# Branch products of attention and merge as three products of rounded parts, in one step of a hybrid decoder on one Trainium2 core

## The reference

```python
n = rms_norm(x, ln1_g)
q_g, k_g, v_g, r_g, a_g, dil_qkv, q_m, gates = split_cols(n @ w_in)
og, gla_state = gla_chunked(qg, kg, vg, lg, gla_s0, gla_chunk)      # gated linear attention
br_gla = og.reshape(B, S, -1) @ w_br_gla                            # 1024 -> 1024
# dilated attention in three groups, mixed per head by the softmax of their denominators
od = jnp.sum(wts[..., None] * jnp.stack(outs, axis=0), axis=0)
br_dil = od.reshape(B, S, -1) @ w_br_dil                            # 512 -> 1024
br_mem = om.reshape(B, S, -1) @ w_br_mem                            # 512 -> 1024
gt = jax.nn.sigmoid(gates.reshape(B, S, N_BRANCH, D))
merged = gt[:, :, 0] * br_gla + gt[:, :, 1] * br_dil + gt[:, :, 2] * br_mem
h = x + merged @ w_out
y = h + peer(rms_norm(h, ln2_g), ...)                               # experts, gathered by row
```

## Time and profile before

| | us |
|---|---|
| median of three runs | 4821.14 |
| the profiled execution, its own time | 4822.78 |
| its span, first to last instruction | 4821.1 |
| PE busy | 4198.3 (87%) |
| VectorE busy | 2510.8 (52%) |
| ScalarE busy | 1744.3 (36%) |
| GpSimd busy | 1589.1 (33%) |
| mean granted clock of TensorE | 0.956 of full speed |

### The profile page before, as it was taken

The page is one execution under the profiler, slowest core; times in us unless marked ns, Lnnn a source line. Parts: engine busy times, 40 slices in busy tenths (PEclk is TensorE's granted clock), DMA queues, the critical chain, the costliest instruction groups (busy, mean ns, idle before and its releaser), DMA issues.

```text
span 4821.1 us, 55456 instructions
## 1 busy us (share of the span) xinstructions
PE 4198.3 (87%) x18644; PEld 2507.5 (52%) x18644; DVE 2510.8 (52%) x5454; ACT 1744.3 (36%) x4662; POOL 1589.1 (33%) x1435
## 2 busy tenths in 40 slices
PE   7999999997555988979889898898898898988987
PEld 6888888886434665444344344343443443443331
DVE  2111111117641763546666666666666666666665
ACT  2111111114411554324444444444444444444443
POOL 0000000004620541124444444444444444444443
PEclk9999999997677999989999999999999999999999
DMA  8898998882457773679999999999999999999998
GB/s 284 285 325 296 320 321 279 293 292 93 134 204 275 239 231 134 222 303 421 421 421 419 411 418 416 417 415 413 416 415 418 415 413 414 418 416 405 416 408 368
DMA packets 317403, 1642.14 MB, mean 341 GB/s; under 512 B 43832, under 2 KB 85656, under 8 KB 175224
## 3 DMA queue, kind: packets, MB, share of 16 engines
q0 software_dynamic: 164720, 1168.36, 59.2%
q1 hardware_dynamic: 116464, 248.64, 15.0%
q10 hardware_dynamic: 35984, 222.30, 13.7%
HBM read 1550.39 MB, written 318.03 MB: 388 GB/s over the span
## 4 chain that ended last, share of the span: by engine, by line
DMA 35%; PE 13%; issue 4%; ACT 4%; DVE 1%; POOL 0%; DVEq 0%; POOLq 0%; ACTq 0%; SPq 0%; PEldq 0%
DMA ex_rows<-scratch_uv,ex_E 35%; PE ex_ps_y L2674 11%; PE ex_ps_q L2622 1%; ACT ex_diag L2376 1%; ACT ex_w L2368 1%; PE ex_ps_t L2587 1%; ACT ex_gel L2364 1%; ACT L2364 0%; ACT L2359 0%; POOL ex_rows L2307 0%; PE ex_ps_y L2668 0%; DVE ex_dots L2521 0%; DVE ex_rows L2521 0%; ACT ex_ex L2359 0%; DMA ex_n2u<-scratch_h 0%
## 5 line engine op out<-in xcount | busy, mean ns | idle before, releaser
L2674 PE MATMUL ex_ps_y<-ex_rows,ex_diag 128*128 128x512 f32 (+1 forms) x4224 | 2030.0, 614 | 310.2 <-ACT ex_diag L2376 285.3
L2521 DVE CUSTOM_DVE_ANT_0 ex_rows<-ex_rows,ex_n2u 128x1024 f32<-128x1024 f32 x1056 | 1294.8, 1226 | 908.7 <-DMA ex_rows<-scratch_uv,ex_E 888.2
L2307 POOL DMA_INDIRECT ex_rows<-scratch_uv,ex_E x1056 | 1233.8, 1168 | 1548.3 <-PE ex_ps_y L2674 1402.9
L2674 PEld LDWEIGHTS ex_ps_y<-ex_rows,ex_diag 128*128 128x128 f32 (+1 forms) x4224 | 739.7, 189 | 1449.0 <-ACT ex_diag L2376 790.0
L2364 ACT ACTIVATE ex_gel<-ex_dots 128x1 f32<-128x1 f32 x1056 | 214.2, 203 | 1425.7 <-DVE ex_dots L2521 1423.1
L410 PE MATMUL pj_ps<-pj_w_hi,pj_nT 128*128 128x470 f32 x3072 | 699.5, 378 | 4.0 <-DVE pj_w_lo L246 2.8
L410 PEld LDWEIGHTS pj_ps<-pj_w_hi,pj_nT 128*128 128x128 f32 x3072 | 580.2, 189 | 87.6 <-issue 8.1
L274 DVE COPY pj_zo<-pj_ps 128x470 f32<-128x470 f32 x96 | 61.3, 646 | 698.8 <-PE pj_ps L410 494.4
L2376 ACT ACTIVATE ex_diag<-ex_ident,ex_w 128x128 f32<-128x128 f32 x1024 | 411.1, 401 | 33.5
L410 PE MATMUL pj_ps<-pj_w_lo,pj_nT 128*128 128x470 f32 x1536 | 362.2, 378 | 0.0
L274 ACT COPY pj_zo<-pj_ps 128x470 f32<-128x470 f32 x96 | 51.8, 553 | 807.1 <-PE pj_ps L410 450.7
(11 more groups left out here) (384 smaller groups left out, 3700.6 us busy)
## 6 DMA issues: line engine op xcount, KB each, us to landing
pj_w<-in_w_in POOLq DMA_DIRECT2D x24, 1880.0 KB, 17.7
scratch_z<-pj_zo SPq DMA_DIRECT2D x192, 235.0 KB, 11.9
scratch_uv<-in_peer_u ACTq DMA_DIRECT2D x8, 4096.0 KB, 25.1
scratch_uv<-in_peer_v ACTq DMA_DIRECT2D x8, 4096.0 KB, 42.5
scratch_uv<-in_peer_u ACTq DMA_DIRECT2D x4, 8192.0 KB, 41.6
scratch_uv<-in_peer_v ACTq DMA_DIRECT2D x4, 8192.0 KB, 72.8
out_dk_s<-in_cache_dil_k ACTq DMA_DIRECT2D x8, 4088.0 KB, 43.0
out_dv_s<-in_cache_dil_v ACTq DMA_DIRECT2D x8, 4088.0 KB, 54.7
```

What stands on the lines that cost most here:

```text
L2307: pool.indirect_dma_start(out=rows[:, p % SLOTS, :], out_offset=None, in_=d["uv"], in_offset=bass.IndirectOffsetOnAxis(ap=E[:, turn % 4, k ...
L2521: nc.vector.tensor_tensor_reduce(out=row, in0=row, in1=n2u[:, tile % 2], scale=1.0, scalar=0.0, op0=ALU.mult, op1=ALU.add, accum_out=dots[ ...
L2674: last = nc.tensor.matmul(y[0:n, 512 * c:512 * c + 512], diag[:, p % DIAGS, 0:n], rows[:, p % SLOTS, D + 512 * c:D + 512 * c + 512], start ...
```

## The change

The branch products of both stages become three products of rounded parts. The weights are no longer used from where they are loaded: w_br_gla goes into wo, and from there ScalarE copies each of its eight slices, rounded, to wb[0], and GpSimd writes the remainder to wb[1]. This is done in turns 1 to 4 by ScalarE (two slices at the end of a turn) and turns 2 to 5 by GpSimd (two slices at the head of a turn). w_br_dil and w_br_mem are then loaded into the two halves of wo at turns 7 and 15, and stay there until the merge, which begins by rounding them: eight copies by ScalarE, four remainders by VectorE and four by GpSimd.

The turned inputs are rounded by ScalarE's copy as before (to ogT[:, 0] and aT[.., 0]), and VectorE subtracts to get the remainder (ogT[:, 1], aT[.., 1]); PE waits for the remainder. The branch stream of attention begins at turn 3 and not 0, and so ends in turn 38; its 48 products a tile (24 for each half) are placed 0, 24, 9 and 15 in the four parts. w_out is not loaded in attention but in the merge, by SyncE at t = 4 ahead of the load of tile 6's rows.

```diff
@@ attend
-    wb = d["wb"] = d["hold_wb"].enter_context(nc.sbuf_tensor("wb", [P, 2 * KD, D], fp32))
+    wb = d["wb"] = [d["hold_wb"].enter_context(nc.sbuf_tensor(n, [P, KD, D], f32r)) for n in ("wb_hi", "wb_lo")]
+    FIRST_BRANCH = 3
+    SPLIT_AT = {n: range(2 * n - 2, 2 * n) for n in range(1, 5)}
+    TERMS = [(a, b, k) for a, b in ((0, 0), (1, 0), (0, 1)) for k in range(KD)]
@@ SyncE
-            weights = [(wb[:, 8:12], "w_br_dil", wb_in), (wb[:, 12:16], "w_br_mem", wb_in), (wo[:], "w_out", wo_in)]
+            weights = [(wo[:, 0:4], "w_br_dil"), (wo[:, 4:8], "w_br_mem")]
-            sp.dma_start(wb[:, 0:8], d["w_br_gla"].rearrange("(k p) n -> p k n", p=P)).then_inc(wb_in, 16)
+            sp.dma_start(wo[:], d["w_br_gla"].rearrange("(k p) n -> p k n", p=P)).then_inc(wb_in, 16)
-                if n % 8 == 7 and n // 8 < 3:
+                if n % 8 == 7 and n // 8 < 2:
+                    sp.wait_ge(wb_lo, KD)
@@ GpSimd
+            def split_weights(k):
+                pool.wait_ge(wb_hi, k + 1)
+                nc.gpsimd.tensor_tensor(wb[1][:, k], wo[:, k], wb[0][:, k], ALU.subtract).then_inc(wb_lo, 1)
             for n in range(LAST + 1):
+                for k in SPLIT_AT.get(n - 1, ()):
+                    split_weights(k)
@@ ScalarE
+            def split_weights(k):
+                act.wait_ge(wb_in, 16)
+                nc.scalar.copy(wb[0][:, k], wo[:, k]).then_inc(wb_hi, 1)
...
+                for k in SPLIT_AT.get(n, ()):
+                    split_weights(k)
@@ VectorE
+            def turned_branch(t, half):
+                dve.wait_ge(ogT_hi, 2 * t + half + 1)
+                ks = slice(4 * half, 4 * half + 4)
+                nc.vector.tensor_tensor(ogT[:, 1, ks, 0:width(t)], ps_b[:].rearrange("p (k t) -> p k t", k=4)[:, :, 0:width(t)],
+                                        ogT[:, 0, ks, 0:width(t)], ALU.subtract).then_inc(ogT_out, 1)
@@ TensorE
-                        pe.wait_ge(wb_in, 16)
+                        pe.wait_ge(wb_hi, KD)
+                if t == 0 and half == 0 and terms[0] == 2 * KD:
+                    pe.wait_ge(wb_lo, KD)
+                for i in terms:
+                    a, b, k = TERMS[i]
+                    last = nc.tensor.matmul(ps_b[0:width(t)], ogT[:, a, k, 0:width(t)], wb[b][:, k, 512 * half:512 * half + 512],
+                                            start=(i == 0), stop=(i == len(TERMS) - 1))
+                if part == 0 and place < 2:
+                    turn_branch(t, place)
                 elif part == 1:
-                    branch_product(t, 0, (range(2, 4), range(4, 5), range(5, 7))[place])
+                    branch_product(t, 0, (range(0, 8), range(8, 16), range(16, 24))[place])
+                elif part == 2 and place:
+                    branch_product(t, 1, (range(0, 4), range(4, 9))[place - 1])
+                elif part == 3:
+                    branch_product(t, 1, (range(9, 14), range(14, 19), range(19, 24))[place])
@@ merge
+                if t == 4:
+                    sp.wait_ge(dil_lo, 4)
+                    sp.wait_ge(mem_lo, 4)
+                    sp.dma_start(wo[:], d["w_out"].rearrange("(k p) n -> p k n", p=P)).then_inc(wo_in, 16)
                 if t + 2 < N:
                     load_a(t + 2)
@@ GpSimd, ahead of its tiles
+            for k in range(4, KD):
+                pool.wait_ge(wb_hi, 2 * (k - 4) + 2)
+                nc.gpsimd.tensor_tensor(wb[1][:, k], wo[:, k], wb[0][:, k], ALU.subtract).then_inc(mem_lo, 1)
@@ ScalarE, ahead of its tiles
+            act.wait_ge(wb_in, 48)
+            for k in (0, 4, 1, 5, 2, 6, 3, 7):
+                nc.scalar.copy(wb[0][:, k], wo[:, k]).then_inc(wb_hi, 1)
@@ VectorE
+            def turned(t):
+                j, n = t % 2, width(t)
+                dve.wait_ge(aT_hi, t + 1)
+                nc.vector.tensor_tensor(aT[:, j, 1, :, 0:n], ps_a[:, j, :, 0:n], aT[:, j, 0, :, 0:n], ALU.subtract).then_inc(aT_out, 1)
+                    if q == 3 and t + 1 < N:
+                        turned(t + 1)
+            for k in range(4):
+                dve.wait_ge(wb_hi, 2 * k + 1)
+                nc.vector.tensor_tensor(wb[1][:, k], wo[:, k], wb[0][:, k], ALU.subtract).then_inc(dil_lo, 1)
             mixed(0)
+            turned(0)
@@ TensorE
-                    for k in range(k0, k1):
-                        last = nc.tensor.matmul(ps_b[0:n, i % BANKS], aT[:, j, k, 0:n], wb[:, KD + k, 512 * c:512 * c + 512],
-                                                start=(k == k0), stop=(k == k1 - 1))
+                    for part, (x, y) in enumerate(PARTS):
+                        for k in range(k0, k1):
+                            last = nc.tensor.matmul(ps_b[0:n, i % BANKS], aT[:, j, x, k, 0:n], wb[y][:, k, 512 * c:512 * c + 512],
+                                                    start=(part == 0 and k == k0), stop=(part == 2 and k == k1 - 1))
```

59 lines of the change are left out of this document (31 added, 28 removed).

## The result

The kernel after is slower: 4839.01 us, the median of seven runs (4833.90 to 4842.44), against 4824.67 for the kernel before (seven runs in the same comparison); ratio 1.0032, 95% interval 1.0021 to 1.0043. The forecast was 4809, faster. The profiled execution took 4841.53 us, its span 4839.9.

The account below looks back on a forecast made before the run. PE was taken to bound attention's dense turns and the merge, VectorE close behind there. Attention -15.6 and merge +3 made -12.6 us on 4822.78, so 4810.2; the runs' median lies 1.6 lower, so 4809, range 4801 to 4818.

Parts of the forecast that it names:

- Start of attention: Attention's first turns: GpSimd's differences and PE's wait for weight copies outweigh PE freed early; +6 us, bounds -5 and +12.
- The Trainium skill's rule: Merge start: VectorE and GpSimd differences block each other, another 3 us; the sum used a measured row instead, some 0.5.
- Start of the merge: Merge's first loads and weight rounding: GpSimd's first scaling and its moves come later, carried on; +2.5 us, bounds 0 and +5.
- Turns 4 to 15: Attention, turn 4 to 16: PE saves 7.5 us over three tiles, counted -6 because VectorE is late once behind the light turn.
- Rival A: Product hidden anyway, VectorE's chain and SyncE end the turns once PE gives way: attention 0, merge +3, 4824 us; chance 0.20.
- w_out in attention: Attention near turn 23: without w_out's load its 10.6 us stall and 2.8 us of slow PE records go; -13.4 us.
- Turns 23 to 36: Attention's keys and memory turns, PE dense: cheaper products give -10.5 us, of which -9.5 was taken.
- End: Attention's turns 36 to 38 now hold the last 48 products: 18.7 us where it was 11.4, +7.3, bounds +4 and +8.
- Merge but for its start: Rest of merge: -2.5 us over tiles 1 to 5 with VectorE the bound, +9 w_out stall, -6 last two tiles.
- the stall for w_out: Merge, t = 4: w_out's load ahead of tile 6's rows makes VectorE wait; +9 us, bounds +3 and +14.
- Rival C: Slower: w_out ahead of the merge's loads stalls two tiles, 26.6 us instead of 9, attention gaining nothing: 4842 us; chance 0.08.
- rival D: Both stages: each rounded part costs a whole fp32 record, +62 us in each stage, some 4935 us; chance 0.02.

Follow-up runs that it names:

- e6: Kernel before with its fp32 stream of branch products three turns later, turns 3 to 38: 4820.5 us, ratio 0.9992.
- e1: Kernel after without GpSimd's eight differences of w_br_gla in attention, PE's work the same: 4827.6 us, ratio 1.0008 to the kernel before.
- e5: e1 with ScalarE's eight weight copies at the end of turns 1 to 3, not 1 to 4: 4818.7 us, ratio 0.9992 to the kernel before.
- e2: Kernel after with all eight weight remainders of the merge computed by VectorE, none by GpSimd: 4835.4 us, ratio 1.0027 to the kernel before.
- v1: Kernel after with two fp32 tiles first, later weight rounding, stream from turn 2, split weight loads, merge remainders on VectorE: 4801.8 us, ratio 0.9958 to before.
- e9: Kernel after without VectorE's subtraction for the remainder of ogT in attention, PE's work the same: 4831.8 us, ratio 1.0014 to the kernel before.
- e7: Kernel after with w_br_dil and w_br_mem loaded in eight pieces in turns 24 to 31: 4835.9 us, ratio 1.0022 to the kernel before.
- e8: Kernel before with two of the eight fp32 products of each half left out in attention: 4805.3 us, ratio 0.9954.
- e4: Kernel after with two of the three parts of each branch product in attention: 4822.4 us, ratio 0.9996 to the kernel before.
- e10: Kernel before with w_out alone moved into the merge, one piece at t = 4: 4821.6 us, ratio 0.9993.

## Why the prediction was wrong

**Start of attention, forecast +6 with bounds of -5 and +12, measured +14.1.** This step failed first. It had PE freed (-8.8 by e6) and a queue of GpSimd at 9.5 us a turn, with a difference at 1.9. GpSimd's turn was 10.4 to 11.3: two differences take 4.7 to 5.7, not 3.8, and VectorE's y took 2 us longer beside each of two of them. And the step named the wait for the eighth copy (1606) without following what stands behind it on PE: the values of unit 0, hence VectorE's output and the next y. That order cost 8.5 in e1, which e5 took away. Counted from attention's first load, the y of units 1 to 4 was forecast for 35, 45, 57 and 67 us and was done at 38.1, 49.4, 65.8 and 75.5: half of the lateness was there before PE's wait, the other half came with it.

**The Trainium skill's rule, counted as "another 3 us" and left out of the sum, was right.** The merge's differences of 3.07 us beside each other and 1.15 alone (e2) are what the Trainium skill, SBUF — State Buffer, section Who interferes with whom, says of VectorE operations with two SBUF inputs: they and GpSimd's reads exclude each other for a whole instruction. The trace agrees, but for a remainder: 1.15 and GpSimd's 2.35 alone (v1) make 3.50, and a pair in turns takes 3.07. The row that was weighed against the rule, VectorE's mean of 1352 ns, looked at one side only. The other side stands in the trace of the kernel before, in GpSimd's crossings: four operations take 1.0 us longer when VectorE's rotary product runs beside them (GpSimd with it, VectorE, GpSimd without it).

```profile
1571.95 3.84 POOL L1357 TENSOR_TENSOR at_t<-at_xr,at_tg 128x256 f32<-128x256 f32 x4
```

```profile
1571.96 1.22 DVE L1483 TENSOR_TENSOR at_t<-at_xr,at_tg 128x1024 f32<-128x1024 f32 x1
```

```profile
1579.27 2.78 POOL L1357 TENSOR_TENSOR at_t<-at_xr,at_tg 128x256 f32<-128x256 f32 x4
```

**Start of the merge, forecast +2.5, measured +7.8** (first scaling at 7.5 us before and 15.3 after, counted from the first load; rows of tile 3 in use at 60.4 and 68.2 us). The sum went by the row and not by the rule; without the block between VectorE and GpSimd (e2) the scaling starts at 11.5 us, so it is 3.8 of the 5.3 us that were missed, and the other 1.5 are not explained. That the delay is handed on to tile 3 whole was forecast rightly.

**Turns 4 to 15, forecast -6, measured +2.1** (over three whole tiles, unit 4 to 16, it is +0.4, and then 16 to 23 is -8.0). "VectorE is late once" behind the light turn was counted at half a microsecond a tile. It was 1.5 to 2 (e9). And the sum had nothing for the loads of w_br_dil and w_br_mem ahead of x, though it saw the same with w_out: as PE gives way, x comes late behind them. ScalarE waits 4.02 us for it behind the load of turn 7, and PE 1.05 for ScalarE's next copy; behind the load of turn 15 ScalarE waits 8.05, and the gap is 3.8 us longer than before. e7, without these two loads there, has 95.6 us from 4 to 15, 4.4 less than before, but it also spares a load that the kernel before had. The reading of the earlier trace rows, PE busy for 38.8 of 40 us, was right for the kernel before: outside the gap with the load e8 gives 0.96 of what PE is spared. It did not hold any more once the new form had given PE less to do and VectorE more: e4, below that, gives 0.15. Rival A, which had VectorE and SyncE end the turns as soon as PE gives way, came close here, and not in the last turns.

**w_out in attention, forecast -13.4, measured -9.7** from unit 15 to 23, -9.2 in e10: the stall went, the 2.8 us for slow records did not come on top. In e10 the gap from unit 22 to 23 fell by 11.8 us and that from 20 to 21 grew by 2.4, with a wait of PE for ScalarE; what is behind that wait stays open. **Turns 23 to 36, forecast -9.5, measured -6.3**: PE-bound, as said (e8 gives 8.5 of 8.6 us, e4 8.8 of some 9), but for the light turns: without VectorE's subtractions (e9) 23 to 33 is 2.7 us shorter. **End, forecast +7.3**: from the begin of turn 36 to the last store's issue it was 18.7 us, as forecast to 0.1.

**Merge but for its start, forecast +0.5, measured -2.0**: a tile took 13.5 to 13.7 us (forecast 13.2 to 13.7, with VectorE as the bound; that it is VectorE is read from the timeline, no run tests it), the stall for w_out was 8.74 (forecast 9), and the product of rounded parts cost what the earlier trace rows said: eight begin 1.83 us before the next group in the merge, 0.229 each, where the forecast had 0.234. The sum: 14.1 + 2.1 - 9.7 - 6.3 + 7.4 (from turn 36 to the merge's first load) = +7.6 and 7.8 - 2.0 = +5.8.

Three terms make 21.5 of the 26.0 us between the forecast of -12.6 and the +13.4 measured, and turned the sign: the start of attention (8.1), the turns 4 to 15 (8.1) and the start of the merge (5.3). Rival C's 4842 comes near the measured 4839, but not by its mechanism, two stalls for w_out: there was one, of 8.74 us. Two readings of the prediction need a word. The 14 records at the start were at half clock only in their first half (granted clock 0.50 in the first 4.4 us, 0.92 in the next 4.2), and rival D's "some 4935" does not follow from +62 us in each stage alone, which give 4945; nothing hangs on either.

## What to carry to other kernels

A step that is added at the start of a pipelined stage is priced by following each wait to what is queued behind it on the waiting engine; here the order within a turn (consumer at its head, producer at its end) cost 8.5 us, about a turn. Do not share element-wise work with two SBUF inputs between VectorE and GpSimd at the same moment. An engine that is busy 97% of a stretch gave 0.6 of what was taken from it, and the loss was one late load: leave out some of its work before paying for a faster form, and look at each gap, not at the stretch alone. When the leading engine gives way, a load queued behind a large one can come late that came in time before.

## What the runs showed of the hardware

A difference of 128x1024 costs VectorE 1.15 us in a row of eight (e2), GpSimd 2.35 alone (v1, median 2358 ns) and each of them 3.07 when both run; a VectorE subtraction of 128x12 took 2.11 beside GpSimd and 0.17 otherwise. Eight products of 128x512 took 3.73 us where PE had waited 4.23 shortly before them, and 1.95 to 2.13 when it was dense:

```profile
1729.42 2.08 PE L1580 MATMUL at_ps_o<-at_v,at_pT 128*128 128x128 f32 x8 [4.23 <-ACT at_pT L1424]
1731.14 3.73 PE L1617 MATMUL at_ps_b<-wb_hi,at_ogT 128*128 128x512 f32 x8
```

The granted clock was 0.54 in the four microseconds from 1731, close to the lower of its two levels, 1.2 GHz. The mean granted clock, with more pauses of PE, fell from 0.92 to 0.89 in attention and from 0.91 to 0.86 in the merge.
